# A three-layer fp32 network on one core: the MLPs' first products turned round, weights stationary, and a busier opening of the second mixer

## The chip, the cores and the metric

The kernel is one launch on one NeuronCore of one Trainium2 chip. The metric is the device time of that launch in microseconds. Before the change it is 2988.74 us (median of 3 runs, 2986.68 to 2989.42).

## The reference, cut to what matters

All is fp32, 256 tokens (S) by 2048 features (D), batch 1.

```
for i in range(2):                     # layer 0: differential attention; layer 1: S5 state-space mixer
    x = x + mixer_i(rmsnorm(x, norm_mix[i]))
    x = x + sqrelu_mlp(rmsnorm(x, norm_mlp[i]), mlp_w1[i], mlp_w2[i])
# then a third, hybrid layer (fox attention and RWKV-7 beside each other, gates, output projection)
def sqrelu_mlp(h, w1, w2):             # w1: 2048 x 8192, w2: 8192 x 2048
    a = relu(h @ w1)
    return (a * a) @ w2
```

The third layer has no MLP of this kind. So the change touches two MLPs, and the S5 mixer's first few microseconds.

## The kernel before, in words

**Products.** A weight matrix streams through SBUF in units of 512 KB. For a product with 512 output columns ("chunk") a unit is two k-tiles: 2 x 128 rows by 512 columns. SP loads it into one of 4 raw slots (`load`, L533). ACT casts it to fp32r as `wH` (`split`, L1760, the cast is L1769), and VectorE forms the rest `wL = raw - wH` (`split`, L2455, L2460). `wH` and `wL` have 4 slots each (SPLIT). The activations have a high and a low part too (`xH`, `xL`, later `hH`, `hL`), stored turned: features in the partitions, 256 tokens in the free dimension. Three fp32r matmuls make one exact enough product: high by high (L985), low by high (L986) and high by low (L992). In `product` (L969) the stationary operand is a 128x128 block of activations, and the moving one is 512 weight columns; a chunk is 8 units x 2 k-tiles x 2 token halves x 3 = 96 matmuls into two PSUM banks `acc[par][0:2]`. Semaphores: `high_done`, `split_done` (a unit is ready), `unit_used` (a unit's slots are free), `acc_free` (a bank was read out).

**MLP.** `mlp` runs 4 blocks (FB) over the 8192 hidden features, one block 2048 wide: 4 chunks h @ w1, then 4 chunks that add this block's share of the output to X. In the first four, ACT takes relu of each bank into `stg` (L1912), VectorE multiplies it by the bank (a * relu(a), the square). The result has tokens in the partitions, but the second product needs it as stationary operand with features in the partitions. So PE turns it: in the middle of the next chunk `turn_stg` (L1017, transposes at L1000) makes 8 transposes of 128x128 into the PSUM tiles `tp`, ACT copies them to `hH` (`high`, L1826) and VectorE forms `hL` (L2517). The first block of an MLP also finishes the normalised input: its last quarter is turned by `lead_turn(3)` inside the first chunk (`lead_first`, L1045); rms scaling is applied to the output, squared (`rstd_sq`). In layer 0 the MLP is written out with S5 set-up work after every chunk (`after`); in layer 1 it is a hardware loop.

**S5 mixer's opening.** After the first MLP's last product PE waits for the row sums (L1255, `choose`), ACT scales the inputs (`permuted`), PE turns them (`inputs_of`, L1270), ACT copies `ut`, PE makes the states' inputs (`states_of`, L1284), VectorE scans, POOL rotates back (L897, L899, L903), PE makes the outputs (`outputs_of`, L1299 to L1301). This goes over 16 groups in a software pipeline; iteration k does `inputs_of(k)`, then `states_of(k-1)`, `outputs_of(k-4)`.

The order of the work is written out by hand in each engine's program; nothing plans it.

Of the kernel before, what the change touches and what calls it, by code (L numbers as in the profile page):

```python
# [21 lines left out]
P = 128  # L22
# [65 lines left out]
SECOND_FILL = 12 + 4 + 8 * FB + 8 + 8 * FB  # L88
# [115 lines left out]
def s5_steps():  # L204

    pe, act, dve, pool = [], [("p", 0)], [], []
    for k in range(S5_B + 5):
        pe += [("u0", k), ("u", k)] * (k < S5_B) + [("g", k - 1)] * (1 <= k <= S5_B) + [("y", k - 4)] * (4 <= k < S5_B + 4)
# [29 lines left out]
def build(nc, I, out):  # L238
    with ExitStack() as ctx:
# [229 lines left out]
        relu_done = sem("relu_done")  # L469
        const_a = sem("const_a")  # L470
# [59 lines left out]
        def _(sp):  # L530
            t = Tally()

            def load(c, j, src):  # L533

                sp.wait_ge(split_done, c * UNITS + (j + 1))
                sp.dma_start(raw[:, j % RAW], src).then_inc(raw_in[j % RAW], 16)
# [429 lines left out]
        def _(pe):  # L966
# [87 lines left out]
            def mlp(after=None, tail=False):  # L1054
                c0, f0, g0 = t.chunk, t.fill, t.group

                def block_of(b, first=None, after=None, tail=False):
                    def turned(c):
                        def mid():
                            pe.wait_ge(acc_free, b * 16 + (2 * (f0 + c) + 6))  # L1060
                            turn_stg(b * 8 + (g0 + 2 * c), c % 2)
                        return mid
                    for c in range(4):
                        product(b * 8 + (c0 + c), b * 8 + (f0 + c), c % 2, xH, xL,
                                mid=turned(c - 1) if c else None, first=first if c == 0 else None)
                        if after:
                            after(c)
                    for c in range(4):
                        product(b * 8 + (c0 + 4 + c), b * 8 + (f0 + 4 + c), c % 2, hH, hL,
                                mid=turned(3) if c == 0 else lead_mid(c - 1) if tail else None,  # L1070
                                first=(lambda j: pe.wait_ge(group_free, b * 8 + (g0 + j + 3))) if c == 0 else None)
# [3 lines left out]
                block_of(0, lead_first, after)  # L1075
# [7 lines left out]
                t.fill += 8 * FB  # L1083
                t.group += 8 * FB
# [161 lines left out]

            t.norm += 1
            pe.wait_ge(acc_free, 2 * t.fill + 4)
# [7 lines left out]
            last.then_inc(rs_summed, 1)  # L1256
            quad = [slice(64 * g, 64 * g + 64) for g in range(2)]
# [499 lines left out]
        def _(act):  # L1757
# [121 lines left out]
            def lead_ends(ready):  # L1879

                split(t.chunk, 1, units=(4, 5))
                lead_high(3)
                split(t.chunk, 1, units=(6, 7))
# [4 lines left out]
            def mlp(after=None, ready=added, tail=False):  # L1888
                lead_ends(ready)
                c0, f0, g0, q0 = t.chunk, t.fill, t.group, t.square  # L1890

                def block_of(b, after=None, entry=False, tail=False):
                    def turned(c):
                        for g in range(2):
                            high(b * 8 + (g0 + 2 * c + g), None, g, hH[:, 4 * c + 2 * g:4 * c + 2 * g + 2])
                    for c in range(8):
                        if c or not entry:
                            split(b * 8 + (c0 + c), 1)
                        if 1 <= c <= 4:
                            turned(c - 1)  # L1900
# [6 lines left out]
                        if c < 4:  # L1907
                            done(b * 8 + (c0 + c))
                            if c >= 2:
                                act.wait_ge(group_done, b * 8 + (g0 + 2 * (c - 1)))  # L1910
                            for m in range(MT):
                                nc.scalar.activation(stg[:, c % 2, m], acc[c % 2][m][:], ACT.Relu).then_inc(relu_done, 1)  # L1912
# [11 lines left out]
                t.fill += 8 * FB  # L1924
                t.group += 8 * FB
# [126 lines left out]
            def s5_scalars(c):  # L2052
# [9 lines left out]
                if c >= 29:  # L2062
                    s5_square(c - 29, t.fill + 28)
                if c == 31:
# [387 lines left out]
        def _(dve):  # L2452
# [101 lines left out]
            def lead_ends():  # L2554

                split(t.chunk, 1, units=(4, 5))
                lead_low(3)
                split(t.chunk, 1, units=(6, 7))
# [32 lines left out]
            def mlp(after=None, tail=None):  # L2591
                lead_ends()
# [3 lines left out]
                c0, f0, h0, q0 = t.chunk, t.fill, t.high, t.square  # L2596

                def block_of(b, after=None, entry=False, tail=None):
                    def turned(c):
                        for g in range(2):  # L2600
                            k = 4 * c + 2 * g
                            low(b * 8 + (h0 + 2 * c + g), g, hH[:, k:k + 2], hL[:, k:k + 2])
                    for c in range(8):
                        if c or not entry:
                            split(b * 8 + (c0 + c), 1)
                        if 1 <= c <= 4:
                            turned(c - 1)
# [4 lines left out]
                        if c < 4:  # L2612

                            for m in range(MT):
                                dve.wait_ge(relu_done, b * 8 + (q0 + 2 * c + m + 1))
                                r = stg[:, c % 2, m]
                                nc.vector.tensor_tensor(r, r, acc[c % 2][m][:], ALU.mult).then_inc(acc_free, 1)
# [894 lines left out]
```

## Time and profile before

| | us |
|---|---|
| median of 3 runs | 2988.74 (2986.68 to 2989.42) |
| the profiled execution | 2983.28 |
| its span on the core | 2981.5 |
| PE busy in the span | 2923.5 (98%), 17561 matmuls |
| VectorE, ScalarE, POOL busy | 1777.8, 1399.8, 368.1 |

TensorE matmuls are pipelined: a record's duration is longer than the distance to the next start, so what one costs in a stream is the distance between starts. In a merged line "1.07 us, x4" of matmuls that last 0.389 each, the distance is (1.07 - 0.389)/3. PE stands for matmuls, PEld for the weight loads that go with them, one for each.

### The profile page before, as it was taken

The page shows a single profiled execution, that of the slowest core. Times are in us where ns is not written, and L with a number is a line of the kernel's source. Part 1 is how long each engine was busy: PE and PEld are TensorE (multiplying, and loading weights), DVE is VectorE, ACT ScalarE, POOL GpSimd, SP SyncE. Part 2 cuts the span into 40 slices and gives each one's busy share as a digit, 9 for nine tenths or more (in the row PEclk, how much of TensorE's full clock was granted, in tenths as well). Part 3 has the DMA queues.
Part 4 walks back from the last instruction along what each step waited for, and adds up shares of the span by engine and source line. Part 5 has one row for each costly group of instructions (what it writes and reads, how often), then busy time and mean ns, then how long its engine had stood idle before and what let it go on. Part 6 is the DMA issues. An engine that isn't in the chain of part 4 may idle for free.

```text
span 2981.5 us, 45318 instructions
## 1 busy us (share of the span) xinstructions
PE 2923.5 (98%) x17561; PEld 2435.9 (82%) x17561; DVE 1777.8 (60%) x2032; ACT 1399.8 (47%) x1949; POOL 368.1 (12%) x424
## 2 busy tenths in 40 slices
PE   9999999999999998999999999999999999998898
PEld 8888788888888887888888888888888888787787
DVE  5555657765766667555555545556644666665765
ACT  5555544343443447444434434344544445653344
POOL 2000010890000776200000000000000001000000
PEclk9999999999999998999999999999999999999999
DMA  7555476775566887566656566665666677661364
GB/s 250 175 170 170 153 208 203 238 230 197 191 208 220 238 257 215 163 193 213 187 190 189 190 185 188 192 186 188 190 178 190 203 206 240 207 197 54 118 211 167
DMA packets 301236, 577.56 MB, mean 194 GB/s; under 512 B 21465, under 2 KB 40153, under 8 KB 299378
## 3 DMA queue, kind: packets, MB, share of 16 engines
q1 hardware_dynamic: 284832, 522.06, 56.2%
q0 software_dynamic: 10992, 43.07, 5.0%
q10 hardware_dynamic: 5218, 9.67, 0.9%
q8 instruction: 142, 2.33, 0.3%
q14 instruction: 52, 0.43, 0.0%
HBM read 546.96 MB, written 21.50 MB: 191 GB/s over the span
## 4 chain that ended last, share of the span: by engine, by line
PE 95%; DVE 2%; ACT 1%; issue 1%; DMA 1%; POOL 0%; ACTq 0%; DVEq 0%; POOLq 0%; SPq 0%
PE acc L985 27%; PE acc L992 27%; PE acc L986 27%; PE tp L1000 2%; PE acc L1711 1%; PE acc L1704 1%; PE acc L1705 1%; DMA raw<-in_mlp_w_dram 1%; PE wk L1284 0%; PE acc L1603 0%; PE acc L1299 0%; PE wk L1613 0%; PE tp L1613 0%; ACT wH L1769 0%; DVE wL L2460 0%
## 5 line engine op out<-in xcount | busy, mean ns | idle before, releaser
L2460 DVE TENSOR_TENSOR wL<-raw,wH 128x1024 fp32r<-128x1024 f32 (+1 forms) x968 | 1203.2, 1251 | 1091.4 <-ACT wH L1769 1089.4
L1769 ACT CAST wH<-raw 128x1024 fp32r<-128x1024 f32 (+1 forms) x968 | 1008.4, 1046 | 1356.0 <-PE acc L992 1184.9
L985 PE MATMUL acc<-wH,xH 128*128 128x512 f32 (+1 forms) x2208 | 864.6, 392 | 0.6 <-issue 0.3
L986 PE MATMUL acc<-wH,xL 128*128 128x512 f32 (+1 forms) x2208 | 855.1, 388 | 1.7 <-issue 1.7
L992 PE MATMUL acc<-wL,xH 128*128 128x512 f32 (+1 forms) x2208 | 587.0, 388 | 0.1
L985 PE MATMUL acc<-wH,hH 128*128 128x512 f32 x1472 | 575.6, 391 | 1.9 <-DVE hL L2517 1.9
L986 PE MATMUL acc<-wH,hL 128*128 128x512 f32 x1472 | 572.8, 389 | 0.0
L985 PEld LDWEIGHTS acc<-wH,xH 128*128 128x128 f32 x2208 | 414.9, 188 | 86.5 <-issue 3.0
L992 PEld LDWEIGHTS acc<-wL,xH 128*128 128x128 f32 x2208 | 412.6, 188 | 85.9 <-DVE wL L2460 0.5
L986 PEld LDWEIGHTS acc<-wH,xL 128*128 128x128 f32 x2208 | 415.0, 188 | 82.6 <-issue 0.5
L992 PE MATMUL acc<-wL,hH 128*128 128x512 f32 x1472 | 393.5, 389 | 0.0
L985 PEld LDWEIGHTS acc<-wH,hH 128*128 128x128 f32 x1472 | 276.5, 188 | 58.9 <-DVE hL L2517 2.4
L992 PEld LDWEIGHTS acc<-wL,hH 128*128 128x128 f32 x1472 | 276.3, 188 | 57.5
L986 PEld LDWEIGHTS acc<-wH,hL 128*128 128x128 f32 x1472 | 276.4, 188 | 56.4
L913 POOL DMA_DIRECT2D prev<-stgs x8 | 4.3, 538 | 1083.5 <-ACT stgs L2256 1083.5
L2517 DVE TENSOR_TENSOR hL<-tp,hH 128x512 fp32r<-128x512 f32 x80 | 51.3, 682 | 6.2 <-ACT hH L1826 6.1
L1704 PE MATMUL acc<-wH,xH 128*128 128x512 f32 x128 | 50.4, 394 | 1.5 <-DVE xL L2517 1.0
L1705 PE MATMUL acc<-wH,xL 128*128 128x512 f32 x128 | 49.9, 389 | 0.0
L1000 PE MATMUL tp<-ident,stgs 128*128 128x128 f32 x384 | 49.6, 272 | 0.0
L1000 PEld LDWEIGHTS tp<-ident,stgs 128*128 128x128 f32 x384 | 44.6, 140 | 6.1
L758 POOL DMA_DIRECT2D sv<-in_b_a_re_dram x1 | 0.5, 545 | 387.7 <-PE tp L1000 387.7
L1826 ACT CAST hH<-tp 128x512 fp32r<-128x512 f32 x80 | 42.7, 586 | 8.0 <-PE tp L1000 8.0
(540 smaller groups left out, 2186.5 us busy)
## 6 DMA issues: line engine op xcount, KB each, us to landing
raw<-in_mlp_w_dram SPq DMA_DIRECT2D x512, 512.0 KB, 3.9
raw<-in_w_in_dram SPq DMA_DIRECT2D x192, 512.0 KB, 4.0
raw<-in_a_w_in_dram SPq DMA_DIRECT2D x96, 512.0 KB, 3.8
raw<-in_b_w_glu_dram SPq DMA_DIRECT2D x64, 512.0 KB, 3.8
raw<-in_a_w_out_dram SPq DMA_DIRECT2D x32, 512.0 KB, 3.8
raw<-in_w_out_dram SPq DMA_DIRECT2D x32, 512.0 KB, 4.2
raw<-in_w_proj_fox_dram SPq DMA_DIRECT2D x16, 512.0 KB, 4.9
raw<-in_w_proj_rwkv_dram SPq DMA_DIRECT2D x16, 512.0 KB, 4.6
```

What stands on the lines that cost most here:

```text
L913: pool.dma_start(prev[1:P], stg[0:P - 1, par]).then_inc(prev_in, 16)
L985: nc.tensor.matmul(bank, aH[:, k, rows], wH[:, j % SPLIT, u, 0:n], start=k == 0, stop=False)
L986: nc.tensor.matmul(bank, aL[:, k, rows], wH[:, j % SPLIT, u, 0:n], start=False, stop=False)
L992: last = nc.tensor.matmul(bank, aH[:, k, rows], wL[:, j % SPLIT, u, 0:n], start=False, stop=k == KT - 1)
L1000: last = nc.tensor.transpose(dst, src, ident[:])
L1704: nc.tensor.matmul(bank, xH[:, k, rows], wH[:, j % SPLIT, u], start=k % 8 == 0, stop=False)
L1705: nc.tensor.matmul(bank, xL[:, k, rows], wH[:, j % SPLIT, u], start=False, stop=False)
L1711: last = nc.tensor.matmul(bank, xH[:, k, rows], wL[:, j % SPLIT, u], start=False, stop=k % 8 == 7)
L1769: nc.scalar.copy(wH[:, j % SPLIT, :, 0:n], raw[:, j % RAW, :, 0:n]).then_inc(high_done, 1)
L1826: nc.scalar.copy(dst, tp[bank][:]).then_inc(group_high, 1)
L2460: nc.vector.tensor_tensor(wL[:, j % SPLIT, :, 0:n], raw[:, j % RAW, :, 0:n], wH[:, j % SPLIT, :, 0:n].bitcast(F32), ALU.subtract).then_inc ...
L2517: nc.vector.tensor_tensor(dL, tp[bank][:], dH.bitcast(F32), ALU.subtract).then_inc(group_free, 1)
```

## The change

What `mlp`'s first products do is turned round. `hidden` replaces `product` for them: the stationary operand is a 128x128 block of the weights, the moving one is all 256 tokens of `xH` or `xL`. The result comes out with hidden features in the partitions and tokens in the free dimension, which is how the second product wants it. A chunk of 512 hidden features is now two half chunks of 256; a half is 4 units of 4 k-tiles by 256 columns, so a unit is still 512 KB, but a loaded row is 1 KB long and not 2 KB. ACT and VectorE evacuate after every half: relu and square on 256 columns, two banks at a time, then `hH` and `hL` straight from `stg`. The transposes, their waits and `tp` are gone from the MLP's chunks. The input's last quarter is turned in unit 1 and needed in unit 3 (before: turned in front of unit 2, needed from unit 6).

In the S5 opening the PE gets matmuls of `ones` by `ones` whose result is not used (`awake`: 15 in the wait before L1255, 4 after it, 3 and then 5 behind `inputs_of` of the first four iterations, 37 in all), and in iterations 1 to 3 `states_of(k-1)` comes ahead of `inputs_of(k)`.

```diff
@@ SP
-                w1v = w1.rearrange("(u k p) n -> u p k n", k=UK, p=P)
+                w1v = w1.rearrange("(u k p) n -> u p k n", k=2 * UK, p=P)
...
-                            load(b * 8 + (c0 + c), j, w1v[j][:, :, bass.ds(b * D + c * NW, NW)])
+                            load(b * 8 + (c0 + c), j, w1v[j % HALF][:, :, bass.ds(b * D + (2 * c + j // HALF) * S, S)], wide=True)
@@ PE
+            def hidden(c, fill, lead=False):
+                for half in range(2):
+                    tile = [acc[half][m][:, 0:S] for m in range(MT)]
+                    pe.wait_ge(acc_free, (fill + half) * 2 + 2)
+                    for i in range(HALF):
+                        j = half * HALF + i
+                        wide = [w[:, j % SPLIT].rearrange("p u (a n) -> p (u a) n", a=2) for w in (wH, wL)]
+                        if lead and j == 0:
+                            pe.wait_ge(group_free, t.lead + 8)
+                        if lead and j == 3:
+                            pe.wait_ge(group_free, t.lead + 10)
+                        pe.wait_ge(high_done, c * UNITS + (j + 1))
+                        for u in range(2 * UK):
+                            k = 2 * UK * i + u
+                            for m in range(MT):
+                                block = wide[0][:, u, m * P:(m + 1) * P]
+                                nc.tensor.matmul(tile[m], block, xH[:, k], start=k == 0, stop=False)
+                                nc.tensor.matmul(tile[m], block, xL[:, k], start=False, stop=False)
+                        if lead and j == 1:
+                            lead_turn(3)
+                        pe.wait_ge(split_done, c * UNITS + (j + 1 + RAW))
+                        for u in range(2 * UK):
+                            k = 2 * UK * i + u
+                            for m in range(MT):
+                                last = nc.tensor.matmul(tile[m], wide[1][:, u, m * P:(m + 1) * P], xH[:, k],
+                                                        start=False, stop=k == KT - 1)
+                        last.then_inc(unit_used, 1)
...
                     for c in range(4):
-                        product(b * 8 + (c0 + c), b * 8 + (f0 + c), c % 2, xH, xL,
-                                mid=turned(c - 1) if c else None, first=first if c == 0 else None)
+                        hidden(b * 8 + (c0 + c), b * 12 + (f0 + 2 * c), lead=lead and c == 0)
...
+            def awake(n):
+                for _ in range(n):
+                    nc.tensor.matmul(acc[0][0][:, 0:P], ones[:], ones[:], start=True, stop=True)
             t.norm += 1
+            pe.wait_ge(acc_free, 2 * t.fill + 2)
+            awake(15)
...
             for k in range(S5_B + 5):
+                if 1 <= k < 4:
+                    states_of(k - 1)
                 if k < S5_B:
                     inputs_of(k)
-                if 1 <= k <= S5_B:
+                if k < 4:
+                    awake(5 if k else 3)
+                if 4 <= k <= S5_B:
                     states_of(k - 1)
@@ ACT
+                    def high_of(h):
+                        act.wait_ge(acc_free, b * 24 + (2 * (f0 + h) + 6))
+                        nc.scalar.copy(hH[:, 2 * h:2 * h + 2], stg[:, h % 2, :, 0:S]).then_inc(hid_high, 1)
+                    def rectified(h):
+                        act.wait_ge(unit_used, (b * 8 + (c0 + h // 2)) * UNITS + (h % 2 * HALF + HALF + SPLIT))
+                        if h >= 2:
+                            act.wait_ge(hid_low, b * 8 + (q0 + h - 1))
+                        for m in range(MT):
+                            nc.scalar.activation(stg[:, h % 2, m, 0:S], acc[h % 2][m][:, 0:S], ACT.Relu).then_inc(relu_done, 1)
...
                         if 1 <= c <= 4:
-                            turned(c - 1)
+                            high_of(2 * c - 1)
+                        if c < 4:
+                            rectified(2 * c)
...
@@ DVE
+                    def low_of(h):
+                        dve.wait_ge(hid_high, b * 8 + (q0 + h + 1))
+                        nc.vector.tensor_tensor(hL[:, 2 * h:2 * h + 2], stg[:, h % 2, :, 0:S],
+                                                hH[:, 2 * h:2 * h + 2].bitcast(F32), ALU.subtract).then_inc(hid_low, 1)
+                    def squared(h):
+                        for m in range(MT):
+                            dve.wait_ge(relu_done, b * 16 + (2 * (q0 + h) + m + 1))
+                            r = stg[:, h % 2, m, 0:S]
+                            nc.vector.tensor_tensor(r, r, acc[h % 2][m][:, 0:S], ALU.mult).then_inc(acc_free, 1)
```

## Rows read from the trace of the kernel before

**Rows 1.** The page: span, busy time, granted clock by 40 slices
```profile
span 2981.5 us, 45318 instructions
PE 2923.5 (98%) x17561; PEld 2435.9 (82%) x17561; DVE 1777.8 (60%) x2032; ACT 1399.8 (47%) x1949; POOL 368.1 (12%) x424
PEclk9999999999999998999999999999999999999999
PE 95%; DVE 2%; ACT 1%; issue 1%; DMA 1%; POOL 0%; ACTq 0%; DVEq 0%; POOLq 0%; SPq 0%
```
**Rows 2.** Who waited for whom, PE, whole span: us, times, longest
```profile
PE tp L1255 <- DVE small L2950: 4.4, 1, 4.4
PE acc L985 <- DVE hL L2517: 1.9, 2, 1.0
```
**Rows 3.** Stretches: length, PE, PEld, DVE, ACT, POOL busy, PEclk, DMA share, GB/s
```profile
952.00:1131.60 179.60, 179.60 (x922) 148.96 (x911) 115.01 (x98) 79.08 (x93) 106.96 (x92) 1.00 0.86 248
1136.00:1154.00 18.00, 14.83 (x200) 12.68 (x200) 12.33 (x24) 13.20 (x49) 11.78 (x15) 0.53 0.88 237
1500.00:1680.00 180.00, 180.00 (x812) 149.42 (x812) 94.18 (x90) 76.18 (x81) 0.00 (x0) 1.00 0.62 189
```
**Rows 4.** Timeline, PE: start, us, line, tile; 512 columns in fp32r
```profile
1301.61 0.39 PE L986 MATMUL acc<-wH,hL 128*128 128x512 f32 x1
1301.84 1.07 PE L992 MATMUL acc<-wL,hH 128*128 128x512 f32 x4
```
**Rows 5.** Timeline, PE: the 8 transposes inside a chunk
```profile
440.20 1.07 PE L992 MATMUL acc<-wL,xH 128*128 128x512 f32 x4
441.11 1.03 PE L1000 MATMUL tp<-ident,stgs 128*128 128x128 f32 x8
441.90 0.48 PE L985 MATMUL acc<-wH,xH 128*128 128x512 f32 x1
442.22 0.40 PE L986 MATMUL acc<-wH,xL 128*128 128x512 f32 x1
```
**Rows 6.** Timeline, PE and its weight loads: fp32r with 200 moving columns
```profile
2204.26 0.61 PE L992 MATMUL acc<-wL,xH 128*128 128x200 f32 x4
2204.16 0.53 PEld L992 LDWEIGHTS acc<-wL,xH 128*128 128x128 f32 x4
```
**Rows 7.** Weight loads round one fp32r matmul of 256 columns (L1423)
```profile
2328.68 0.19 PEld L1423 LDWEIGHTS wk<-nct,pick 128*128 128x128 f32 x1
2328.89 0.19 PEld L985 LDWEIGHTS acc<-wH,xH 128*128 128x128 f32 x1
2329.01 0.19 PEld L986 LDWEIGHTS acc<-wH,xL 128*128 128x128 f32 x1
...
2330.17 0.19 PEld L985 LDWEIGHTS acc<-wH,xH 128*128 128x128 f32 x1
```
**Rows 8.** DMA issues: count, KB each, median us to landing
```profile
raw<-in_mlp_w_dram SPq DMA_DIRECT2D x512, 512.0 KB, 3.9
ft<-f_scratch SPq DMA_DIRECT2D x16, 256.0 KB, 2.8
```
**Rows 9.** Timeline, VectorE and ScalarE, at the start of the first MLP
```profile
410.74 1.28 DVE L2541 TENSOR_TENSOR xn<-X,gains 128x512 f32<-128x512 f32 x2
413.72 1.07 ACT L1826 CAST xH<-tp 128x512 fp32r<-128x512 f32 x2
414.99 1.28 DVE L2517 TENSOR_TENSOR xL<-tp,xH 128x512 fp32r<-128x512 f32 x2
```
**Rows 10.** Timeline, all engines, the S5 mixer's opening
```profile
1136.04 0.58 PE L1255 MATMUL tp<-small,choose 128*128 128x4 f32 x4 [4.42 <-DVE small L2950]
1139.01 0.37 ACT L2106 COPY ut<-acc 128x256 f32<-128x256 f32 x1
1139.52 0.98 PE L1270 MATMUL acc<-ident,up 64*128 64x64 f32 x4 [0.55 <-ACT ut L2106]
1140.43 1.97 PE L1284 MATMUL wk<-ut,gt 64*64 64x64 f32 x32
1146.06 1.27 POOL L897 TENSOR_TENSOR zz<-rc,rt 128x512 f32<-128x512 f32 x1 [4.90 <-DVE rc L2989]
1154.81 0.70 PE L1270 MATMUL acc<-ident,up 64*128 64x64 f32 x4 [0.61 <-ACT ut L2106]
1155.44 1.15 PE L1284 MATMUL wk<-ut,gt 64*64 64x64 f32 x32
```

More of the change, by code:

```diff
@@ L207, in s5_steps @@
     for k in range(S5_B + 5):
-        pe += [("u0", k), ("u", k)] * (k < S5_B) + [("g", k - 1)] * (1 <= k <= S5_B) + [("y", k - 4)] * (4 <= k < S5_B + 4)
+        turns, states = [("u0", k), ("u", k)] * (k < S5_B), [("g", k - 1)] * (1 <= k <= S5_B)
+        pe += (states + turns if k < 4 else turns + states) + [("y", k - 4)] * (4 <= k < S5_B + 4)
         pe += [("h", (k - 6) // 2)] * (k >= 6 and k % 2 == 0)
@@ L1054, in mlp, with block_of @@
             def mlp(after=None, tail=False):
[L1055 to L1062, printed above, removed]
+                c0, f0, q0 = t.chunk, t.fill, t.square
+                def block_of(b, lead=False, after=None, tail=False):
                     for c in range(4):
-                        product(b * 8 + (c0 + c), b * 8 + (f0 + c), c % 2, xH, xL,
-                                mid=turned(c - 1) if c else None, first=first if c == 0 else None)
+                        hidden(b * 8 + (c0 + c), b * 12 + (f0 + 2 * c), lead=lead and c == 0)
                         if after:
@@ L1068, in block_of @@
                     for c in range(4):
-                        product(b * 8 + (c0 + 4 + c), b * 8 + (f0 + 4 + c), c % 2, hH, hL,
-                                mid=turned(3) if c == 0 else lead_mid(c - 1) if tail else None,
-                                first=(lambda j: pe.wait_ge(group_free, b * 8 + (g0 + j + 3))) if c == 0 else None)
+                        product(b * 8 + (c0 + 4 + c), b * 12 + (f0 + 8 + c), c % 2, hH, hL,
+                                mid=lead_mid(c - 1) if c and tail else None,
+                                first=(lambda j: pe.wait_ge(hid_low, b * 8 + (q0 + j + 1))) if c == 0 else None)
                         if after:
                             after(4 + c)
-                block_of(0, lead_first, after)
+                block_of(0, True, after)
                 if after:
@@ L1877, in lead_root, with lead_ends @@
                 nc.scalar.activation(std, ss, ACT.Sqrt, bias=eps, scale=1.0 / D).then_inc(std_done, 1)
-            def lead_ends(ready):
-                split(t.chunk, 1, units=(4, 5))
+            def lead_ends(ready, n=2):
+                split(t.chunk, 1, units=range(4, 4 + n))
                 lead_high(3)
-                split(t.chunk, 1, units=(6, 7))
+                split(t.chunk, 1, units=range(4 + n, 8))
                 ready(3)
@@ L1888, in mlp @@
             def mlp(after=None, ready=added, tail=False):
[L1889 to L1890 removed]
+                lead_ends(ready, 1)
+                c0, f0, q0 = t.chunk, t.fill, t.square
                 def block_of(b, after=None, entry=False, tail=False):
[L1893 to L1895 removed]
+                    def high_of(h):
[7 more added lines that the diff above has]
+                            nc.scalar.activation(stg[:, h % 2, m, 0:S], acc[h % 2][m][:, 0:S], ACT.Relu).then_inc(relu_done, 1)
                     for c in range(8):
@@ L1907, in block_of @@
                         if c < 4:
[L1908 to L1912, printed above, removed]
+                            high_of(2 * c)
+                            rectified(2 * c + 1)
                         if after:
@@ L2552, in lead_rstd, with lead_ends @@
                 nc.vector.reciprocal(rstd, std).then_inc(rstd_done, 1)
-            def lead_ends():
-                split(t.chunk, 1, units=(4, 5))
+            def lead_ends(n=2):
+                split(t.chunk, 1, units=range(4, 4 + n))
                 lead_low(3)
-                split(t.chunk, 1, units=(6, 7))
+                split(t.chunk, 1, units=range(4 + n, 8))
                 lead_rstd()
@@ L2595, in mlp @@
                 dve.wait_ge(scale_own, t.scale)
-                c0, f0, h0, q0 = t.chunk, t.fill, t.high, t.square
+                c0, f0, q0 = t.chunk, t.fill, t.square
                 def block_of(b, after=None, entry=False, tail=None):
[L2599 to L2602, printed above, removed]
+                    def low_of(h):
[7 more added lines that the diff above has]
+                            nc.vector.tensor_tensor(r, r, acc[h % 2][m][:, 0:S], ALU.mult).then_inc(acc_free, 1)
                     for c in range(8):
@@ L2612, in block_of @@
                         if c < 4:
[L2614 to L2617, printed above, removed]
+                            low_of(2 * c)
+                            squared(2 * c + 1)
                         else:
```

39 lines of the change are left out of this document (22 added, 17 removed).

## The prediction, made before the changed kernel was run

> **What bounds the kernel now.** I read the page first: PE is busy for 2923.5 of 2981.5 us, and 95% of the chain of work that ended last is PE; the granted clock is full nearly everywhere [rows 1]. The reader should then ask what PE waits for: the longest waits are 4.4 us before L1255 and two of 1.9 us together for `hL` [rows 2]. The table by stretches settles it for the MLPs: between 1500 and 1680 us PE is busy 180.00 of 180.00 us, VectorE 94, ScalarE 76, and the DMA engines 62% [rows 3]. So inside an MLP the time is the number of matmuls times the distance between their starts. Anything that takes work from VectorE or ScalarE is worth nothing there; only the distance and the count decide. The one place where the clock is low is 1136 to 1154 us, at 0.53 of full, which is about the lower level of 1.2 GHz for nearly all of it [rows 3].
>
> **The change part by part.** The profiled execution took 2983.28 us, 5.5 below the median of the runs shown (2988.74). The sum is made against 2983.28, and the 5.5 is added again at the end.
>
> *1. The first products, before.* 2 MLPs x 4 blocks x 4 chunks = 32 chunks, each 96 matmuls, 3072 in all. Four of 512 columns take 1.07 us with 0.389 for the last one, so (1.07 - 0.389)/3 = 0.227 from start to start [rows 4]; I use 226.7 ns. That is 696.4 us.
>
> *2. The first products, after.* The same number of columns passes, in 6144 matmuls of 256 columns, each with a weight load of its own: the records show one load per matmul everywhere, 17561 of each [rows 1]. So all hangs on one number, X, the distance between fp32r matmuls of 256 columns. 1 ns of X is 6.1 us. No stretch of the trace has such a stream. The bounds:
> - Low end: transposes of 128 columns follow each other at (1.03 - 0.27)/7 = 109 ns [rows 5], though 128 columns at 2.4 GHz would be 53; a weight load of 128 columns sets that. 6144 x 109 = 669.7 us, -26.7.
> - A closer low row: fp32r with 200 columns, (0.61 - 0.273)/3 = 112 ns, and its loads (0.53 - 0.188)/3 = 114 [rows 6]. 200 columns would be 83 ns, so this too is the pace of the loads. 6144 x 112 = 688.1, -8.3.
> - By columns: 226.7/2 = 113.3 ns, 0.0 by construction.
> - A single one: L1423 has 256 fp32r columns between other shapes. The next weight loads start 0.12 us apart (2328.89 and 2329.01) [rows 7], 118 in the trace's own nanoseconds and the same at all eight such places. But it stands in a disturbed stretch: behind it five 512-column matmuls take (2330.17 - 2329.01)/5 = 232 ns each, 5 more than in a stream. Less 5 it is 113, by ratio 118 x 226.7/232 = 115.
> - High end: 512 columns at 2.4 GHz are 213.3 ns, the stream needs 13.4 more. If these are paid per matmul and not per column, X = 106.7 + 13.4 = 120: 737.3 us, +40.9.
>
> I take X = 114.5, between the readings of rows 7, a little above the pace by columns because loads (112 to 114) and columns (113.3) are so near that each small slip of one shows. 6144 x 114.5 = 703.5 us: **+7.1**.
>
> The Trainium skill ("TensorE: Matmul & The Clock Gate", "Back-to-back issue gap" and "LDWEIGHTS") gives N/2.4 + 2.5 ns for a warm matmul and P/1.2 ns for a load of P columns; that would be 109 and 107 ns here, an estimate by that page. Its 216 ns for 512 columns are not what the trace has (227), so for fp32r I let the trace decide; it is a rival below. The same page ("What happens when you issue a matmul") says that loads have a read port of their own and don't slow the stream. By that rule the 13.4 ns are no cost of the load, which speaks against 120. No row here shows the ports.
>
> *3. The transposes go.* From the start of the four L992 to the transposes 440.20 to 441.11 is four distances; from 441.11 to the L986 at 442.22 it is 1.11 us, of which one matmul is 0.227 [rows 5]: 0.883 us for 8 transposes. All of it is on the bound engine. 32 x 0.883 = **-28.3**. The bounds are narrow (8 x 109 = 0.872 to 0.89). ScalarE's and VectorE's copies read `stg` in place of `tp`, same size; hidden.
>
> *4. Evacuation by halves.* ScalarE and VectorE now have 11 us (half a chunk) to empty a bank pair before PE wants it again, before it was 22. The work is two relus and two products of 256 columns each, some 2 us. In the order of their queues they stand right behind the split of unit 7, which waits for unit 3, the half's own end, so nothing is late; in front of PE's next half lie three or four split units, 8 us. For `hH`/`hL` half 7 is needed in unit 7 of chunk 4, 19 us in, and is ready at about 13 (split of unit 7 at 10.9, copy, subtraction). Cost 0. If the cover is gone (VectorE's S5 set-up behind a chunk in layer 0, where it is busy 64% [rows 3]) a wait of 1 us in each of 64 halves is +64; I see no row that makes one. The 1.9 us for `hL` [rows 2] I leave at 0: not all in an MLP.
>
> *5. Loads with 1 KB rows.* A 512 KB unit has 512 rows, not 256. The nearest row is `ft`, 256 rows of 1 KB in 2.8 us, against 3.9 for 256 rows of 2 KB [rows 8]. So a new unit lands in at most 2 x 2.8 = 5.6 us; a raw slot comes round every 4 x 2.72 = 10.9 us. Hidden: 0. If a 1 KB row cost as much as a 2 KB one, a share of 0.62 would be 1.24 and the 256 loads would be the bound: 0.24 x 2.72 x 256 = +167; rows 8 speak against it.
>
> *6. MLP openings, two.* `lead_turn(3)` now comes 4.6 us into the first chunk (unit 0 and two thirds of unit 1), before 5.4. The chunk began at 407.07, so 411.7; the last gain product ends at 410.74 + 1.28 = 412.02 [rows 9], +0.3. Transposes to 413.0, two casts (1.07), then two subtractions (1.28) overlapping: `xL` complete near 415. PE reaches unit 3 at 416. With 0.1 to spare for semaphores: **+0.4 each, +0.8**. Ends: 0 and +3 (if VectorE's split of unit 4 falls between).
>
> *7. S5 opening.* POOL is the slow engine there once it starts: L897 runs 16 times and starts at 1146.06, after a wait of 4.90 [rows 10]. So what counts is how early the first states are made. `states_of(0)` starts at 1140.43, behind `inputs_of(1)`, though `ut` was ready at 1139.38; in the new order it starts 1.0 us sooner. At the full clock it takes 1.15 and not 1.97 us, `inputs_of` 0.70 and not 0.98 [rows 10]: 0.8 + 0.3, and about 0.2 on L1255. If `awake` keeps the clock: -2.3. If not: -0.8. The 15 fill 1.6 of a wait of 4.4 us; those behind `inputs_of(0)` (3 x 0.11) lie beside ScalarE's `ut` (0.37); the others lie ahead of PE waits. PE's queue holds nothing else that they delay. I take **-2.3**, with ends 0 and -4.
>
> Sum: +7.1 - 28.3 + 0.8 - 2.3 = **-22.7**; 2983.28 - 22.7 = 2960.6; plus 5.5 = **2966 us**.
>
> **The rivals.** All share -29.8 (parts 3, 6, 7).
> - R1, X = 118 as the bare reading of rows 7: +28.6 - 29.8 = -1.2, 2987.5, no change. For: eight such readings agree. Against: their neighbours are slow too.
> - R2, the slower side: the excess over the columns is paid per matmul. Place: every one of the 6144; price X = 120, +40.9 - 29.8 = +11, about 3000 us. It decides from X = 119.2 on. For: nothing in the stream of one size excludes it. Against: 118 in a stretch where 512 columns have an excess of 18.7 leaves only 11.3 for 256.
> - R3, X = 109, the loads' pace of rows 5: -26.7 - 29.8 = -56.5, 2932 us. This is what the skill's gap rule gives. For: columns and load are both below it at full clock. Against: 112 with only 200 columns.
> - R4, a half waits for its bank or for a load (parts 4 and 5): +0.5 us in each of 64 halves turns the gain into +9, 2998 us. Against: PE has no wait of this kind now, and there is cover of 8 us.
> - R5, the change doesn't do what it says: the granted clock still falls after L1255. It shifts the sum by 1.5 us only and is inside the forecast.
>
> **How the numbers follow.** Forecast (X 112.5 to 116.5, -40 to -10 in all) 0.64; R1 0.10; R2 0.09; R3 0.13; R4 0.04. The forecast's own range is 2950 to 2979. The range for 8 in 10 reaches to 2943, on the way to R3, and to 2992, past R1. Under 0.2% (6 us) this kernel's times can't be told from no change. Faster: 0.64 + 0.13 + a little of R1 = 0.79; same: most of R1, 0.08; slower: R2 and R4, 0.13.
>
> **What would show it.** The distance between the starts of `hidden`'s matmuls in its four-in-a-row lines: 114.5 right, 118 R1, 120 R2, 109 R3. No `tp<-ident,stgs` in the MLPs, 256 fewer of L1000. A half chunk should last 96 x X = 11.0 us, back to back. No PE wait for `acc` by VectorE's squares or ScalarE's relus; DMA share in the first products up by some hundredths, landing under 6 us. PEclk 1.0 from 1136 on and L897's first start some 2.3 us sooner, counted from the last product's end. I am wrong if the distance lies outside 112 to 117, or if PE shows idle time in the MLPs.

## The result: slower by 0.36%, and the profile after

The changed kernel takes 2997.27 us, the median of 8 runs (2993.56 to 3001.54); the kernel before, on the same chip, 2987.56 (8 runs, 2983.07 to 2989.42). The ratio is 1.0036 [1.0027, 1.0045], which is +10.8 us. (Here and below, microseconds beside a ratio, and the brackets with them, are the ratio and its interval times the median of the kernel before in the same set of runs. They can be some 1 to 2 us off the difference of the medians, here 9.7.) The prediction was 2966 us, "faster"; the range ended at 2992. What came is the rival R2, whose price for the products is right; that its total of +11 fits to a microsecond is in part luck, as the last point on the prediction shows.

The page of the changed kernel (span, busy time, the chain by engine and by line, two groups, the loads), for [rows 1] and [rows 8]:

```profile
span 2999.7 us, 51274 instructions
PE 2945.9 (98%) x20451; PEld 2580.0 (86%) x20451; DVE 1796.1 (60%) x2096; ACT 1405.5 (47%) x2013; POOL 370.8 (12%) x424
PE 92%; DMA 3%; DVE 2%; ACT 2%; issue 1%; SPq 0%; ACTq 0%; DVEq 0%
L1020 PE MATMUL acc<-xH,wH 128*128 128x256 f32 x2048 | 503.1, 283 | 0.8 <-ACT wH L1811 0.8
L1028 PE MATMUL acc<-xH,wL 128*128 128x256 f32 x2048 | 287.6, 283 | 0.0
raw<-in_mlp_w_dram SPq DMA_DIRECT2D x512, 512.0 KB, 3.9
```

PE waits 0.8 us in all for its 6144 new matmuls, and the loads land as before. So the new products are neither starved nor held up; the time is in the distance between them. The timeline of PE and the table of stretches (columns as in [rows 3]):

```profile
1430.81 0.64 PE L1028 MATMUL acc<-xH,wL 128*128 128x256 f32 x4
1431.29 0.28 PE L1020 MATMUL acc<-xH,wH 128*128 128x256 f32 x1
1431.41 0.28 PE L1021 MATMUL acc<-xL,wH 128*128 128x256 f32 x1
1431.53 0.28 PE L1020 MATMUL acc<-xH,wH 128*128 128x256 f32 x1
...
1453.37 1.12 PE L1028 MATMUL acc<-xH,wL 128*128 128x256 f32 x8
```
```profile
408.30:1139.25 730.95, 730.05 (x4940) 668.43 (x4939) 490.35 (x534) 312.56 (x377) 260.62 (x250) 1.00 0.72 219
1407.21:1494.53 87.32, 87.32 (x730) 87.32 (x729) 47.01 (x56) 42.22 (x59) 0.45 (x1) 1.00 0.66 205
1154.90:1165.10 10.20, 9.63 (x118) 8.68 (x120) 5.34 (x10) 3.23 (x13) 7.33 (x6) 0.50 0.51 146
```

Starts are 0.12 us apart: 1431.29, .41, .53. In the eight in a row it is (1.12 - 0.283)/7 = 0.120; the median over each of the three lines (L1020, L1021, L1028) is 120 ns. The second row lies inside a block's first products (87.32 us are 7.6 half chunks of 96 matmuls): PE is busy for all of it. The third is where the clock is at its lower level now: behind the opening, not in front of it.

By stage, from the starts of the matmuls in the profiled executions (us):

| from - to | before | after | new products alone |
|---|---|---|---|
| first MLP's first product - L1255 (L1292 after) | 728.97 | 735.66 | 734.82 |
| from there to the GLU's first product | 68.09 | 71.22 | 68.32 |
| from there to the fox scores (holds the second MLP) | 1115.78 | 1120.51 | 1120.50 |
| from there to the last matmul | 653.71 | 656.13 | 655.13 |

The last column is the experiment `mlp_only` below. Each MLP lost 5 to 7 us; it should have won 10. The change doesn't touch the last stage. Most of its 2.4 us are the clock: the changed kernel has two stretches of 3.4 us at 0.50 there, the kernel before none in its profiled execution. Not all of it is: `mlp_only` has no such stretch there either and is 1.4 longer.

### The profile page after: what moved, and what is told of

Its sections match the earlier page's. It is cut to its first block, busy times and chain, and to the rows that moved or that the text cites. A ratio compares the mean times of both kernels' runs of the same rounds, so it can differ in the third digit from the quotient of the medians.

```text
span 2999.7 us, 51274 instructions
## 1 busy us (share of the span) xinstructions
PE 2945.9 (98%) x20451; PEld 2580.0 (86%) x20451; DVE 1796.1 (60%) x2096; ACT 1405.5 (47%) x2013; POOL 370.8 (12%) x424
## 4 chain that ended last, share of the span: by engine, by line
PE 92%; DMA 3%; DVE 2%; ACT 2%; issue 1%; SPq 0%; ACTq 0%; DVEq 0%
PE acc L991 19%; PE acc L992 19%; PE acc L998 19%; PE acc L1028 8%; PE acc L1020 8%; PE acc L1021 8%; DMA raw<-in_mlp_w_dram 2%; PE tp L1036 1%; PE acc L1753 1%; PE acc L1746 1%; PE acc L1747 1%; DVE wL L2508 1%; ACT wH L1811 1%; PE wk L1322 1%; PE acc L1337 0%
## 5 line engine op out<-in xcount | busy, mean ns | idle before, releaser
L1020 PE MATMUL acc<-xH,wH 128*128 128x256 f32 x2048 | 503.1, 283 | 0.8 <-ACT wH L1811 0.8
L1021 PE MATMUL acc<-xL,wH 128*128 128x256 f32 x2048 | 502.6, 283 | 0.0
L991 PE MATMUL acc<-wH,xH 128*128 128x512 f32 (+1 forms) x1184 | 463.9, 393 | 0.4 <-ACT wH L1811 0.4
L992 PE MATMUL acc<-wH,xL 128*128 128x512 f32 (+1 forms) x1184 | 457.2, 387 | 0.0
L1020 PEld LDWEIGHTS acc<-xH,wH 128*128 128x128 f32 x2048 | 393.0, 192 | 1.8 <-ACT wH L1811 1.0
L1021 PEld LDWEIGHTS acc<-xL,wH 128*128 128x128 f32 x2048 | 393.1, 192 | 0.4 <-issue 0.2
L998 PE MATMUL acc<-wL,xH 128*128 128x512 f32 (+1 forms) x1184 | 313.1, 386 | 0.0
L1028 PE MATMUL acc<-xH,wL 128*128 128x256 f32 x2048 | 287.6, 283 | 0.0
L1028 PEld LDWEIGHTS acc<-xH,wL 128*128 128x128 f32 x2048 | 264.2, 192 | 0.0
L998 PEld LDWEIGHTS acc<-wL,xH 128*128 128x128 f32 x1184 | 220.4, 188 | 45.5
```

Source lines behind the costliest of these rows:

```text
L991: nc.tensor.matmul(bank, aH[:, k, rows], wH[:, j % SPLIT, u, 0:n], start=k == 0, stop=False)
L992: nc.tensor.matmul(bank, aL[:, k, rows], wH[:, j % SPLIT, u, 0:n], start=False, stop=False)
L998: last = nc.tensor.matmul(bank, aH[:, k, rows], wL[:, j % SPLIT, u, 0:n], start=False, stop=k == KT - 1)
L1020: nc.tensor.matmul(tile[m], block, xH[:, k], start=k == 0, stop=False)
L1021: nc.tensor.matmul(tile[m], block, xL[:, k], start=False, stop=False)
L1028: last = nc.tensor.matmul(tile[m], wide[1][:, u, m * P:(m + 1) * P], xH[:, k], start=False, stop=k == KT - 1)
```

## The experiments

Theory F, formed on this result: an fp32r matmul costs its columns at 2.4 GHz and 13.3 ns more, whatever its width. Rival C: the cost goes by columns (0.443 ns each), and 120 has another cause (banks, the order of operands, the alternation of `xH` and `xL`). The openings are a question of their own.

**m_columns**, a kernel of its own that has nothing of the network: 64 back-to-back matmuls of each kind, with nothing to wait for.

```diff
+            for i in range(64):
+                last = nc.tensor.matmul(acc[i % 4][:, 0:256], wr[:, i % 8], xr[:, i % 4, 0:256], start=True, stop=True)
```

This stands there once for each of 512, 448, 384, 320, 288, 256, 224, 200, 160 and 128 columns, then with the same weights, with the moving data in two runs, in bf16, in plain fp32 (32 matmuls) and with 64 weight columns. The kernel was executed once.

> A kernel of its own, without the network: streams of 64 matmuls on full 128x128 weights, each stream on a source line of its own, moving columns 512, 448, 384, 320, 288, 256, 224, 200, 160, 128 in fp32r, then the same weights again, moving data in two runs, bf16, plain fp32, and fp32r with 64 weight columns. Theory F (a fixed 13.3 ns per fp32r matmul on top of its columns): 227, 200, 173, 147, 133, 120 ns down to 256 columns, then 112 (the pace of the weight loads) from 224 on. Rival C (the excess goes with the columns, 0.443 ns each, and 256 is slow only because columns and load collide at nearly the same length): 227, 198, 170, 142, 127, 120. The two part at 384 and 320: 173 against 170, 147 against 142. If the excess belongs to fp32r, bf16 has 216 and 109 for 512 and 256; if it belongs to every change of weights, bf16 has 227 and 120 too, and the stream with the same weights stays at 120 only if a load is issued all the same.

Groups of instructions of this kernel (busy time, mean ns of one); the distance is (busy - mean)/63, and the starts in the trace give it to a tenth:

```profile
L55 PE MATMUL acc<-xr,wr 128*128 128x512 f32 x64 | 14.7, 389 | 0.0
L61 PE MATMUL acc<-xr,wr 128*128 128x384 f32 x64 | 11.3, 335 | 0.0
L64 PE MATMUL acc<-xr,wr 128*128 128x320 f32 x64 | 9.5, 309 | 0.0
L70 PE MATMUL acc<-xr,wr 128*128 128x256 f32 x64 | 7.8, 283 | 0.0
L76 PE MATMUL acc<-xr,wr 128*128 128x200 f32 x64 | 7.3, 274 | 0.0
L97 PE MATMUL acc<-xb,wb 128*128 128x512 bf16 x64 | 14.0, 379 | 0.0
L100 PE MATMUL acc<-xb,wb 128*128 128x256 bf16 x64 | 7.2, 273 | 0.0
L115 PE MATMUL acc<-xr,wr 128*64 128x256 f32 x64 | 7.4, 276 | 0.0
```

| moving columns, fp32r | 512 | 448 | 384 | 320 | 288 | 256 | 224 to 128 |
|---|---|---|---|---|---|---|---|
| distance, ns | 226.7 | 202.7 | 173.4 | 146.7 | 131.7 | 120.0 | 111.6 |
| above columns / 2.4 GHz | 13.4 | 16.0 | 13.4 | 13.4 | 11.7 | 13.3 | - |

F holds and C falls: by columns 384 would be 170 and 320 would be 142. F is not exact: 448 lies 2.7 above it and 288 lies 1.6 below. Below 256 a floor of 111.6 takes over, the same for four widths. The same weights in each matmul change nothing (120.0, 226.7; each still has its load), nor does moving data in two runs. In bf16 it is 215.8 and 109.2. That is what the Trainium skill ("TensorE: Matmul & The Clock Gate", "Back-to-back issue gap") gives, N/2.4 + 2.5 ns: right here for bf16, not for fp32r, whose fixed part is five times as large. The rule's form, a fixed part per matmul, was right and speaks against splitting a matmul; the prediction took only its figure from it, for R3.

**mlp_only**: the changed kernel with the opening of before.

```diff
-            awake(15)
...
-                if 1 <= k < 4:
-                    states_of(k - 1)
```

> The change without the opening of the S5 mixer (no ones, old order of states and inputs). Theory F: 6144 x 120.0 - 3072 x 226.7 = +40.9, transposes -28.3, about +1 at the two MLP starts: +13 to +14 us against before, and the opening is then worth about -3. Rival O (the opening in its new order costs some us, as the profiled run of the changed kernel suggests with +3): this kernel is at +7.

Measured 1.0035 [1.0022, 1.0049], +10.4 us [6.6, 14.6] (2995.44; 2985.44 before). So the loss is in the products, and the new opening is worth nothing that shows beside them. F's sum is 40.9 - 28.3 = +12.6, and +13 to +14 was expected with the two MLP starts. The interval holds that, and also the +7 of rival O, so this run alone doesn't part the two; `open_only` does.

**open_only**: the kernel before with the new opening and nothing else.

```diff
+            awake(15)
...
+                if 1 <= k < 4:
+                    states_of(k - 1)
```

> The kernel before with the new opening alone. Theory F with an opening that does what I forecast: -2 to -4 us against before, clock 1.0 through the opening. Rival O: +1 to +4 us, because states_of(2) in front of inputs_of(3) now waits for the gt load and holds the inputs behind it, and the clock still falls.

Measured 0.9989 [0.998, 0.9999], -3.3 us. That is inside what was expected, and rival O (+1 to +4) is out. Its opening, in the table of stretches, against [rows 3]; below it the changed kernel's timeline there:

```profile
1136.00:1154.00 18.00, 15.37 (x244) 13.29 (x244) 13.16 (x29) 13.41 (x51) 11.54 (x14) 1.00 0.91 250
```
```profile
1139.47 3.51 PE L1280 MATMUL acc<-ones 128*128 128x128 f32 x30
1143.96 0.58 PE L1292 MATMUL tp<-small,choose 128*128 128x4 f32 x4 [0.97 <-DVE small L3002]
1147.41 1.15 PE L1322 MATMUL wk<-ut,gt 64*64 64x64 f32 x32
1152.22 1.27 POOL L903 TENSOR_TENSOR zz<-rc,rt 128x512 f32<-128x512 f32 x1 [3.13 <-DVE rc L3041]
1155.35 1.97 PE L1322 MATMUL wk<-ut,gt 64*64 64x64 f32 x32 [1.77 <-DMA gt<-g_scratch]
1157.25 1.01 PE L1308 MATMUL acc<-ident,up 64*128 64x64 f32 x4
```

The clock is full where it was 0.53, and POOL's first `zz` comes 8.26 us after the row sums' matmul (1152.22 - 1143.96) against 10.02 before [rows 10]: -1.8, where -2.3 was forecast. `awake(15)` shows as 30 records: a plain fp32 matmul is two. So the 15 fill 3.5 us and not the 1.6 of the prediction, and 0.97 us of the wait are left. In the changed kernel there is a loss beside it. The states, now first in the queue, wait 1.77 us for `gt`, and `inputs_of(3)` stands behind them. (In `open_only` this wait is 0.9 us.)

**joined**: the new products, but `xH` and `xL` in one tile, so that one 512-column matmul on `wH` does what two of 256 did. ScalarE copies the second half out, VectorE adds it, takes max and square.

```diff
-                                nc.tensor.matmul(tile[m], block, xH[:, k], start=k == 0, stop=False)
-                                nc.tensor.matmul(tile[m], block, xL[:, k], start=False, stop=False)
+                                nc.tensor.matmul(acc[half][m][:], block, xHL[:, :, k], start=k == 0, stop=False)
```

> mlp_only with one edit more: xH and xL lie in one tile, and one matmul of 512 moving columns (256 of xH, 256 of xL) takes the place of the two of 256 on wH; the two halves of the bank are added afterwards (ScalarE copies one half, VectorE adds, and max-times squares). Theory F: 2048 x 226.7 + 2048 x 120.0 = 710.1 us against 737.3, -27 against mlp_only and -13 to -14 against before. Rival C, where 256 is slow only by collision: the wL part may stay at 120 and the joined part is 227 all the same, so it says the same here; what would refute both is a joined matmul above 227 because its moving data lie in two runs, or a wait for VectorE, which has 0.7 us more in every half (then -10 or less against mlp_only).

Measured 0.999 [0.9981, 0.9999], -3.0 us: 13.4 better than `mlp_only`, where the fixed part alone makes 2048 x 13.3 = 27. In its timeline the 512s are not at 227:

```profile
1431.69 2.00 PE L1020 MATMUL acc<-xHL,wH 128*128 128x512 f32 x8
1433.53 1.12 PE L1027 MATMUL acc<-xHL,wL 128*128 128x256 f32 x8
```

(2.00 - 0.389)/7 = 230. That explains about half of what is missing (`m_loads` below). By stage, `joined` against `mlp_only`: the second MLP is 10.4 us shorter (1110.11 against 1120.50), the first only 2.9 (731.91 against 734.82), and the opening, where the clock is at 0.50 for 23.9 us in this execution and not 17.1, is 2.5 longer. So the rest is mainly in the first MLP. ScalarE waited there for the weights. The first fence has its waits from 408 to 1135 us in `joined`, the second the same in the kernel before; the third has PE's waits for ScalarE in `joined`. The columns are us in total, times, longest.

```profile
ACT wH L1798 <- DMA raw<-in_mlp_w_dram: 140.2, 70, 10.5
```
```profile
ACT wH L1769 <- DMA raw<-in_mlp_w_dram: 82.1, 37, 5.8
```
```profile
PE acc L1020 <- ACT wH L1798: 4.0, 2, 2.2
```

**m_loads**, again a kernel of its own: fewer weight columns, and streams that mix widths. Theory L: the 13.3 ns are time that the weight load takes from the stream, so fewer weight columns give less. P: it belongs to each matmul. S: after a change of shape a stream needs some matmuls to settle.

```diff
+            for g in range(16):
+                for i in range(8):
+                    nc.tensor.matmul(acc[i % 2][:, 0:512], wr[:, i % 8], xr[:, i % 4, 0:512], start=True, stop=True)
+                for i in range(8):
+                    nc.tensor.matmul(acc[i % 2][:, 0:256], wr[:, i % 8], xr[:, i % 4, 0:256], start=True, stop=True)
```

> A kernel of its own, without the network: fp32r streams of 96 matmuls with 512, 384 and 256 moving columns, each with 128, 96, 64 and 32 weight columns; then mixed streams. m_columns gave 13.3 ns over the columns at every width from 256 to 512 with full weights, but 6.7 with 64 weight columns at 256. Theory L (the load of fp32r weights takes the time from the stream, in proportion to the weight columns): the excess at 256 and 384 is 13.3, 10, 6.7, 3.3 ns for 128, 96, 64, 32 weight columns, and the same at 512. Rival P (paid per matmul, whatever is loaded): 13.3 everywhere, and the 113 of m_columns was the settling after another stream. Mixed streams: the joined kernel's 512-column matmuls took 231 ns and not 227 behind each group of 256. Theory S (a stream of 512 takes about eight matmuls to settle after another width): 8 and 8 has 231 and 120, 16 and 16 has some 229 on average, and after two plain fp32 ones the first eight take 231 to 232 and the other sixteen 227. Rival: 227 throughout here, and the 4 ns come from the other engines of the full kernel.

Groups of it (96 each, one execution), and its timeline in the mix of eights:

```profile
L67 PE MATMUL acc<-xr,wr 128*128 128x384 f32 x96 | 16.8, 334 | 0.0
L76 PE MATMUL acc<-xr,wr 128*32 128x384 f32 x96 | 16.8, 336 | 0.0
L79 PE MATMUL acc<-xr,wr 128*128 128x256 f32 x96 | 11.7, 283 | 0.0
L88 PE MATMUL acc<-xr,wr 128*32 128x256 f32 x96 | 11.0, 276 | 0.0
```
```profile
251.37 2.00 PE L95 MATMUL acc<-xr,wr 128*128 128x512 f32 x8
253.21 1.12 PE L97 MATMUL acc<-xr,wr 128*128 128x256 f32 x8
```

With 128, 96, 64 and 32 weight columns: 256 moving columns take 120.0, 115.9, 113.3, 113.3; 384 take 173.3, 175.0, 173.3, 173.3; 512 take 226.7, 230.0, 229.9, 231.7. L falls at 384, P alone at 256: what the 13.3 ns are stays open. S holds. In the mix of eights the distances repeat as 234, 236, 228, 232, 231, 227, 227, 226 for the 512s and 114, 119, 120, 120, ... for the 256s; in a mix of sixteens the first eight are the same and the rest 227. So S is right that a stream has to settle, though it takes five matmuls and not eight. The very first 256s after 512s read below their settled 120, and the first 512s read above their 227. The 256 of [rows 7] stands behind plain fp32 ones. `m_columns` has such a place too: behind plain fp32 its 256s go 118, 116, 119, 119, 121, 116, 118 (after a first one of 306) and only then stay at 120. That is the 118 that [rows 7] had shown.

**second_only**: `joined`, but in the second MLP alone (the first keeps the old form), since the first MLP's stretch has the busier DMA queues (0.86 against 0.62 in [rows 3]).

```diff
-            stream_mlp(I["mlp_w1"][1], I["mlp_w2"][1])
+            stream_wide(I["mlp_w1"][1], I["mlp_w2"][1])
```

> The kernel before, with the joined form (one matmul of 512 moving columns on wH, of 256 on wL) in the second MLP alone, where no S5 set-up shares VectorE and the DMA engines; the first MLP and the opening are as before. In the joined kernel the second MLP's stretch was 5.7 us shorter than before and the first one's 2.9 us longer. Theory (joined is good by 5 to 6 us where nothing disturbs it; the first MLP lost it in four late loads of about 2 us each): -5 to -7 us against before. Rival (the gain of the second stretch was that execution's luck): 0 to -2 us.

Measured 0.9966 [0.9954, 0.9978], -10.2 us [-13.7, -6.6]; 2977.69 (2975.66 to 2981.42). It beats both kernels. The stage with the second MLP is 1109.82 us against 1115.78. By rows: 1024 pairs (a 512 and a 256) of 349.2 ns (the mix of eights in `m_loads`) are 357.6 us against 348.2, and the transposes give 14.1: -4.7 from PE, and the stage shows -6.0. That is the theory's -5 to -7. The runs give more than the stage accounts for; what the rest is stays open. Their interval ends at -6.6.

**two_turns**: the kernel before, with 2 of the 8 transposes in each MLP chunk (three quarters of `hH` and `hL` are made from older data). It measures part 3 alone.

```diff
-                                  tp[g][:, k, m * P:m * P + P]) for k in range(2) for m in range(MT)])
+                                  tp[g][:, k, m * P:m * P + P]) for k in range(some) for m in range(some)])
...
-                            turn_stg(b * 8 + (g0 + 2 * c), c % 2)
+                            turn_stg(b * 8 + (g0 + 2 * c), c % 2, some=1)
```

> The kernel before with 2 transposes where the MLPs had 8 in each chunk (192 of 256 left out; three quarters of hH and hL are then old data). Theory (the prediction's term, 0.883 us for 8, all on PE's path): 192 x 0.109 = -21 us. Rival (something else waits behind them, for instance hL for the next product): less than -17.

Measured 0.9918 [0.9906, 0.9931], -24.5 us [-28.1, -20.6]. Six of eight go, so a transpose is worth 24.5/192 = 0.128 us [0.107, 0.146]; the forecast had 0.883/8 = 0.110, which the interval holds. All of it was on the path.

**rows_1k**: the kernel before, its first weights loaded as 4 k-tiles by 256 columns (so products over the wrong weights). It measures part 5 alone.

```diff
-                            load(b * 8 + (c0 + c), j, w1v[j][:, :, bass.ds(b * D + c * NW, NW)])
+                            load(b * 8 + (c0 + c), j, w1v[j % HALF][:, :, bass.ds(b * D + (2 * c + j // HALF) * S, S)], wide=True)
```

> The kernel before with the MLPs' first weights loaded as the changed kernel loads them, 4 k-tiles by 256 columns with rows of 1 KB, and used as if they were 2 by 512 (so these products have the wrong weights; the work is the same). Theory D (the 1 KB rows make some loads late in the first MLP, where POOL's set-up traffic shares the DMA engines; the joined kernel had four PE waits of 1 to 2.5 us there): +2 to +8 us against before, all of it before the S5 mixer, nothing in the second MLP. Rival (they land in time as the prediction says): -1 to +1.

Measured 1.0009 [1.0001, 1.0018], +2.7 us. In its timeline (PE, then ScalarE) and table of stretches:

```profile
436.12 1.07 PE L995 MATMUL acc<-wL,xH 128*128 128x512 f32 x4
440.90 0.50 PE L988 MATMUL acc<-wH,xH 128*128 128x512 f32 x1 [3.71 <-ACT wH L1772]
439.80 1.04 ACT L1772 CAST wH<-raw 128x1024 fp32r<-128x1024 f32 x1 [9.53 <-DMA raw<-in_mlp_w_dram]
```
```profile
436.00:441.00 5.00, 1.29 (x7) 0.75 (x5) 0.12 (x1) 1.04 (x1) 0.00 (x0) 1.00 1.01 284
441.00:446.00 5.00, 5.00 (x15) 3.95 (x16) 4.55 (x9) 4.72 (x7) 0.00 (x0) 0.66 0.49 149
```

One load came so late that PE ran dry, in a stretch where the DMA engines are full (1.01), and right behind it the clock is low for a while (second row, a mean of 0.66). The median landing says nothing of such a place. But this is the slowest of the twelve runs (2997.09). Six of them take 2986.5 to 2989.1 us, as most runs of the kernel before do (median 2987.00); the other six take 2992.3 to 2997.1, with a mean granted clock of 0.993 or 0.994 each. So the +2.7 is the average of runs that lose nothing and runs that lose 5 us and more. In the profiled one the loss isn't only where theory D puts it: the first MLP is 5.6 us longer than before, but the stage with the second is 2.7 longer, with one more stretch of 3.4 us at 0.50, and the last stage is 3.6 longer, with three. How much of the +2.7 is the rows and how much the clock is not shown.

**ones_only** (the matmuls of ones, old order), **second_open** (`second_only` with the new opening) and **second_ones** (`second_only` with the ones, old order) share these edits with `open_only`:

```diff
+            pe.wait_ge(acc_free, 2 * t.fill + 2)
+            awake(15)
...
+            awake(4)
...
+                if k < 4:
+                    awake(5 if k else 3)
```

> The kernel before with the matmuls of ones in the opening, but the old order of states_of and inputs_of. If the order is what gains (POOL's first L897-like product 1.8 us sooner in open_only, with 1.1 of it from the order): about -2 us against before, 1 less than open_only. If the order costs (states_of(2) waits for its gt load in front of inputs_of(3)): -3 us or better.

> second_only with the new opening as well. If the two are independent: -8 to -10 us against before (opening -3.3 as measured alone). If the opening is only as good as the clock, which fell all the same in the changed kernel's profile: no more than second_only.

> The best parts together: the joined form in the second MLP alone (-10 us measured alone) and the matmuls of ones in the opening with the old order (-6.6, measured alone). If they add up: -14 to -17 us against before, about 2971. If the opening's gain depends on where the clock's fall comes: -10 to -13.

Measured: `ones_only` 0.9978 [0.9968, 0.9988], -6.6 us; `second_open` 0.9964 [0.9951, 0.9978], -10.8; `second_ones` 0.9963 [0.995, 0.9976], -11.1 (2977.82; 2974.97 to 2979.7). Alone, the new opening is worth 3 us and the ones without the new order 7; the intervals, [-6.0, -0.3] and [-9.6, -3.6], overlap. So -6.6 fits the expectation that the order costs something, but what the order adds or costs can't be told. Beside `second_only` (-10.2) neither adds what can be told. The three best kernels can't be told from each other.

Where do the 6.6 us of `ones_only` lie? In its profiled execution the opening (from the row sums' matmul to the GLU's first product) is not shorter at all, 68.58 us against 68.09, but there the clock still falls:

```profile
1136.00:1154.00 18.00, 17.07 (x213) 14.81 (x215) 9.44 (x20) 13.43 (x49) 8.90 (x12) 0.81 0.80 221
```

In the profiled executions of `open_only`, `second_open` and `second_ones` it doesn't fall in the opening, which takes 66.39, 66.68 and 66.12 us (68.42 in `second_only`, where it falls for 20.5 us). The runs' mean granted clocks say that the profiled `ones_only` (0.998) is not its typical run: six of the nine have 0.999, and all nine have 0.997 to 0.999, where the 14 of the kernel before have 0.994 to 0.996. A mean of 0.999 is at most 9 us at half clock (an estimate from the rounding), and the profiled executions have 5 to 7 of them at the very end of the kernel; that leaves no room for the 6.8 us in the opening. So a clock that stays up in the opening goes with an opening that is about 2 us shorter, and by this estimate it stays up in most runs with the ones. The rest of the 6.6 is not placed. Two microseconds are too few to be seen beside `second_only`, whose interval is 7 us wide: that the parts don't add up is not shown, only that -14 to -17 did not come (`second_ones`' interval, [-14.9, -7.2], just reaches it).

## Why the prediction was wrong, point by point

- *Part 2 failed, at X.* "I take X = 114.5": it is 120.0, so +40.9 and not +7.1. The bounds held 120 and R2 named its mechanism, price and deciding point (119.2), but it had 0.09. The step that failed is "Less 5 it is 113": I took a neighbour's slowness off a reading of 118. `m_loads` shows that the two have opposite signs. Behind a change of width the first 512s are slow (234, 236) and the first 256s are fast (114, 119; behind plain fp32, as in [rows 7], 118 and 116). The 118 was a transitional reading, and the settled one lies above it. What the runs showed in its place is 120.0, in the changed kernel and in a stream with nothing else. R2's own "Against" was the same step, and is void for the same reason.
- *Part 2's high end was sound arithmetic.* 512 columns leave 13.4 ns unexplained; six widths in m_columns show 11.7 to 16.0, four of them 13.3 or 13.4. No width between 256 and 512 ran in a stream of the kernel before, and at 200 the floor of 112 hides the fixed part, so only bounds could be had. I gave the middle 0.64 and R2 0.09; the rows didn't support such a difference.
- *Part 3 held.* -28.3 forecast; `two_turns` gives -24.5 for three quarters of it, and its interval holds the forecast's three quarters, -21.2.
- *Part 4 held.* PE waits 0.8 us for a cast and never for a bank; a half chunk is 96 x 0.120 = 11.5 us.
- *Part 5 was a little off.* 0 forecast, +2.7 [0.3, 5.4] measured, with the doubt said under `rows_1k`. The working compared medians; what costs in the profiled execution is a single late load where the queues are full. The far bound (+167) is out.
- *Part 6 held.* In the first MLP `lead_turn(3)` waits 0.27 us for its gain product where +0.3 was forecast (the loads of its transposes, below), and nothing behind it is late. In the second MLP PE waits 1.5 us there, against 0.9 before: +0.6 for +0.4.

```profile
413.31 0.85 PEld L1036 LDWEIGHTS tp<-ident,xn 128*128 128x128 f32 x8 [0.27 <-DVE xn L2589]
```

- *Part 7 held in its mechanism* (clock full at the start, first `zz` 1.8 sooner), -3.3 alone, but nothing beside the new products. R5 came half: in the changed kernel's profiled execution the clock falls 11 us after L1292 (1154.9 - 1143.96), for 10.2 us, where before it fell at once for 17.1; and the states wait for `gt`. With the same opening in `open_only` it does not fall.
- *The sum by measured terms*: +40.9 - 28.3 + 0.8 + 2.7 = +16.1 without the opening, against +10.4 [6.6, 14.6]. With the transposes as `two_turns` has them (256 x 0.128 = -32.7) it is +11.7. R2's +11 had the transposes 4 us too small, the loads at nothing and 2.3 us for an opening that showed nothing in the total: these misses cancel, and that is luck. The sign rests on X alone: with X = 114.5 either sum is well below zero.

## What to carry to other kernels

Count matmuls, not only columns: each fp32r matmul pays 12 to 16 ns on top of its 256 to 512 columns, so halving the moving size costs 6% here (226.7 to 2 x 120.0), more than the transposes that it saved. A price per instruction read from one instance between other shapes is no price for a stream, and must not be corrected by its neighbours; measure a stream, or let both bounds keep their chances. Where turning a product round saves work, keep its moving side at 512 (here by laying the high and the low part side by side), and put it where the weights come early. A profiled execution is one of many: compare its time and granted clock with the other runs before its waits are taken for the kernel's.

## What the runs showed of the hardware that I had not expected

- After a change of width the first five 512s of an fp32r stream are off: 234, 236, 228, 232, 231, then 227, 227, 226. One 512 and one 256 together take 349.2 ns in groups of eight, 347.9 in groups of sixteen and 353.5 one by one in turns, where 346.7 would be the settled sum.
- The floor for 224 to 128 moving columns is 111.6 ns in fp32r with full weights. In bf16 128 columns take 55.8.
- With 64 or fewer weight columns 256 moving ones take 113.3 and not 120.0, but 384 stay at 173.3, and 512 get slower (230 to 232).
- A plain fp32 matmul is two instructions: 430 ns for 512 columns, 216 for 256, each of the two.
- The time of a run goes with its mean granted clock also from run to run of one kernel: in 52 runs of the kernel before, the 12 at 0.994 have a mean of 2989.4 us, the 26 at 0.995 one of 2986.4, the 12 at 0.996 one of 2984.9.
